# The additions of the norms' squares in GpSimd's program, between the low halves of the weights

## The reference

```python
h = rms_norm(x, norm_g[l, 0]) * (1 + sc1) + sh1
m = even_mixer(h, ...) if l % 2 == 0 else odd_mixer(h, ...)
x = x + g1 * rms_norm(m, norm_g[l, 1])
h = rms_norm(x, norm_g[l, 2]) * (1 + sc2) + sh2
x = x + g2 * rms_norm(mlp(h, mlp_w1[l], mlp_w2[l]), norm_g[l, 3])

def rms_norm(x, g):                       # float32
    y = x * lax.rsqrt(jnp.mean(x * x, axis=-1, keepdims=True) + EPS)
    return y * g
def mlp(h, w1, w2):
    return jnp.square(jax.nn.relu(h @ w1)) @ w2          # 1024 -> 4096 -> 1024
```

## Time and profile before

| what | value |
|---|---|
| time, median of 3 runs | 3595.27 us (3594.14 to 3598.88) |
| profiled execution | 3591.43 us, of which the span of the instructions 3589.8 us |
| TensorE matmul busy | 3171.7 us (88%), mean granted clock 0.927 |
| VectorE busy | 1320.4 us (37%) |
| ScalarE busy | 951.1 us (26%) |
| GpSimd busy | 628.1 us (17%) |

### The profile page before, as it was taken

One profiled execution on the slowest core, in us unless ns is written; L12 is line 12 of the kernel. 1 busy time (PEld: TensorE's weight loads), 2 busy tenths in 40 slices (PEclk: granted clock), 3 DMA queues, 4 the chain that ended last, 5 costly groups with the idle time before them and its releaser, 6 DMA issues. The chain is left out here.

```text
span 3589.8 us, 44989 instructions
## 1 busy us (share of the span) xinstructions
PE 3171.7 (88%) x17605; PEld 2783.1 (78%) x17605; DVE 1320.4 (37%) x2055; ACT 951.1 (26%) x1404; POOL 628.1 (17%) x368
## 2 busy tenths in 40 slices
PE   4898888889777688899999998879778899999998
PEld 2883333369656478899999998867568899999997
DVE  4126651111297417322222227119516422222225
ACT  3016663200231224212122223213324212222211
POOL 1211111121000021221112221117021112222210
PEclk7899999989889589999999999989779999999998
DMA  5110005421231232111111122130242111111112
GB/s 210 53 48 20 1 25 175 153 65 47 100 107 54 78 109 74 48 42 36 40 47 47 47 85 70 52 109 5 66 128 67 43 45 47 47 47 47 41 36 106
DMA packets 236954, 238.89 MB, mean 67 GB/s; under 512 B 8003, under 2 KB 194807, under 8 KB 236565
## 3 DMA queue, kind: packets, MB, share of 16 engines
q1 hardware_dynamic: 221701, 205.73, 18.2%
q0 software_dynamic: 5120, 16.78, 1.5%
q10 hardware_dynamic: 10016, 14.78, 1.2%
HBM read 207.74 MB, written 29.99 MB: 66 GB/s over the span
## 5 line engine op out<-in xcount | busy, mean ns | idle before, releaser
L614 PE MATMUL PS<-trunk_x_hi,trunk_w_hi 128*128 128x364 f32 x2208 | 739.1, 335 | 87.1 <-DVE trunk_x_lo L1242 31.9
L615 PE MATMUL PS<-trunk_x_lo,trunk_w_hi 128*128 128x364 f32 x2208 | 736.3, 333 | 0.0
L616 PE MATMUL PS<-trunk_x_hi,trunk_w_lo 128*128 128x364 f32 x2208 | 735.2, 333 | 0.0
L831 POOL TENSOR_TENSOR trunk_w_lo<-trunk_w_raw,trunk_w_hi 128x1024 fp32r<-128x1024 f32 x128 | 307.0, 2398 | 1318.4 <-ACT trunk_w_hi L1009 1228.1
L614 PE MATMUL PS<-hidden,trunk_w_hi 128*128 128x364 f32 x1536 | 508.0, 331 | 0.0
L615 PE MATMUL PS<-hidden,trunk_w_hi 128*128 128x364 f32 x1536 | 505.9, 329 | 0.0
L616 PE MATMUL PS<-hidden,trunk_w_lo 128*128 128x364 f32 x1536 | 505.5, 329 | 0.0
L614 PEld LDWEIGHTS PS<-trunk_x_hi,trunk_w_hi 128*128 128x128 f32 x2208 | 423.6, 192 | 89.2 <-DVE trunk_x_lo L1242 32.4
L615 PEld LDWEIGHTS PS<-trunk_x_lo,trunk_w_hi 128*128 128x128 f32 x2208 | 423.7, 192 | 0.0
L616 PEld LDWEIGHTS PS<-trunk_x_hi,trunk_w_lo 128*128 128x128 f32 x2208 | 422.8, 191 | 0.0
L1260 DVE TENSOR_TENSOR M<-M,PS 128x364 f32<-128x364 f32 x336 | 178.3, 532 | 440.9 <-PE PS L616 440.9
(11 more groups left out here) (369 smaller groups left out, 4266.3 us busy)
## 6 DMA issues: line engine op xcount, KB each, us to landing
trunk_w_raw<-mlp_w SPq DMA_DIRECT2D x128, 512.0 KB
M<-cache_sb_k SPq DMA_DIRECT2D x64, 256.0 KB, 3.0
big<-cache_sb_v POOLq DMA_DIRECT2D x64, 256.0 KB, 3.3
x_scratch<-x_new ACTq DMA_DIRECT2D x9, 1456.0 KB, 5.9
hgrn_pairs_ada_w<-ada_w SPq DMA_DIRECT2D x24, 512.0 KB
x_new<-x_scratch SPq DMA_DIRECT2D x6, 1456.0 KB, 11.8
trunk_x_old<-x_scratch SPq DMA_DIRECT2D x6, 1456.0 KB, 10.9
setup_ada_w<-ada_w SPq DMA_DIRECT2D x16, 512.0 KB, 7.2
```

The lines of the kernel that those rows point to most:

```text
L614: pe.matmul(out, hi, xh, start=first, stop=False)
L615: pe.matmul(out, hi, xl, start=False, stop=False)
L616: return pe.matmul(out, lo, xh, start=False, stop=last)
L831: pool.tensor_tensor(wl[:, u % 4, :], raw[:, u % 2, :], wh[:, u % 4, :].bitcast(F32), ALU.subtract).then_inc(s_lo, 1)
```

## The change

The function `tree` moves from VectorE's program to GpSimd's, with the same two additions on the same data, the same waits and the same semaphores; all 21 calls go with it (six in each stretch of layer 0 and in the first of layer 1, three at the end). GpSimd's loop over the MLP's groups starts at group 1 instead of 0, and group 0's eight units are written out, with trees in between.

```diff
--- before.py
+++ after.py
@@ -823,15 +823,45 @@
                 pool.tensor_tensor(wl[:, u % 4, :], raw[:, u % 2, :], wh[:, u % 4, :].bitcast(F32),
                                    ALU.subtract).then_inc(s_lo, 1)
 
+            def tree(j, n, c):
+                w = squares_of(j, n, c)
+                pool.wait_ge(s_q[j][n], (c + 1) * (2 if n else 1))
+                pool.tensor_tensor(w[:, 0:4], w[:, 0:4], w[:, 4:8], ALU.add).then_inc(s_tree[j][n], 1)
+                pool.wait_ge(s_tree[j][n], 2 * c + 1)
+                pool.tensor_tensor(w[:, 0:2], w[:, 0:2], w[:, 2:4], ALU.add).then_inc(s_tree[j][n], 1)
+
             for u in range(8):
                 low_weights(u)
-            with pool.Fori(0, G) as g:
+            tree(0, 0, 0)
+            tree(0, 1, 0)
+            tree(0, 0, 1)
+            for u in range(8, 12):
+                low_weights(u)
+            tree(0, 0, 2)
+            tree(0, 1, 1)
+            tree(0, 1, 2)
+            for u in range(12, 16):
+                low_weights(u)
+            with pool.Fori(1, G) as g:
                 for u in range(8):
                     pool.wait_ge(s_hi, g * 8 + (8 + u + 1))
                     pool.tensor_tensor(wl[:, u % 4, :], raw[:, u % 2, :], wh[:, u % 4, :].bitcast(F32),
                                        ALU.subtract).then_inc(s_lo, 1)
-            for n in range(units_next):
-                low_weights(8 + 8 * G + n)
+            u0 = 8 + 8 * G
+            tree(1, 0, 0)
+            if final:
+                tree(1, 0, 1)
+                tree(1, 0, 2)
+                return
+            tree(1, 1, 0)
+            tree(1, 0, 1)
+            for n in range(4):
+                low_weights(u0 + n)
+            tree(1, 0, 2)
+            tree(1, 1, 1)
+            tree(1, 1, 2)
+            for n in range(4, units_next):
+                low_weights(u0 + n)
 
         @block.tensor
         def _(pe):
@@ -1178,13 +1208,6 @@
 
         @block.vector
         def _(dve):
-            def tree(j, n, c):
-                w = squares_of(j, n, c)
-                dve.wait_ge(s_q[j][n], (c + 1) * (2 if n else 1))
-                dve.tensor_tensor(w[:, 0:4], w[:, 0:4], w[:, 4:8], ALU.add).then_inc(s_tree[j][n], 1)
-                dve.wait_ge(s_tree[j][n], 2 * c + 1)
-                dve.tensor_tensor(w[:, 0:2], w[:, 0:2], w[:, 2:4], ALU.add).then_inc(s_tree[j][n], 1)
-
             def recip(j, n, c):
                 dve.wait_ge(s_rt[j][n], c + 1)
                 at = slice(NBK * n + 4 * c, NBK * n + 4 * c + 4)
@@ -1268,12 +1291,9 @@
                 dve.wait_ge(s_sh, c + 1)
                 dve.tensor_tensor(col(XL, c), col(M, c), col(XH, c).bitcast(F32), ALU.subtract).then_inc(s_sl, 1)
 
-            tree(0, 0, 0)
             recip(0, 0, 0)
             scaled(0, 0)
             residual(0, 0)
-            tree(0, 1, 0)
-            tree(0, 0, 1)
             recip(0, 1, 0)
             normed(0, 0)
             recip(0, 0, 1)
...
@@ -1351,9 +1365,7 @@
                     dve.wait_ge(s_rT, i + 1)
                     dve.tensor_copy(rows_of(i)[0:n_rows(i), HALF:D], PS[0:n_rows(i), 2 * (i % 3) + 1, :]).then_inc(s_rv, 1)
                 return
-            tree(1, 1, 0)
             down(e, 2, 0)
-            tree(1, 0, 1)
             down(e, 2, 1)
             recip(1, 1, 0)
...
```

More of the change, by code:

```diff
@@ L1284, in _ @@
             hidden(0, 0, 0)
-            tree(0, 1, 1)
             hidden(0, 0, 1)
-            tree(0, 0, 2)
             hidden(0, 0, 2)
@@ L1297, in _ @@
             hidden(0, 1, 0)
-            tree(0, 1, 2)
             hidden(0, 1, 1)
@@ L1320, in _ @@
                 down(e, 0, f)
-            tree(1, 0, 0)
             down(e, 1, 0)
@@ L1345, in _ @@
                 down(e, 2, 7)
-                tree(1, 0, 2)
                 recip(1, 0, 2)
@@ L1370, in _ @@
             residual(1, 1)
-            tree(1, 1, 1)
-            tree(1, 0, 2)
             recip(1, 1, 1)
@@ L1379, in _ @@
             residual(1, 2)
-            tree(1, 1, 2)
             recip(1, 1, 2)
```

## The result

| | median, us | runs | ratio to before, 95% interval |
|---|---|---|---|
| before | 3597.07 | 3594.14 to 3604.61, 4 | |
| after | 3658.59 | 3651.55 to 3666.03, 4 | 1.0172 (1.0151 to 1.0193) |

Before has one run more here than in the table of its profile. The change makes the kernel 61.5 us slower, 1.7%; 55.5 us and with them 3650 were forecast.

A forecast was written before the change was run, and what follows sets the result against it. A tile-to-tile norm chain was taken to bound the kernel, with the trees' latency on it, not VectorE's load. 23.0 + 22.7 + 9.8 = 55.5 us on 3591.43 gave 3646.9, with the median's 3.8 about 3650; range 3628 to 3663.

The forecast's parts named there:

- more standing: Rival: VectorE's hidden-row steps also stand beside trees (0,1,1), (0,1,2) and reach TensorE's wait; +10 us, 3660; chance 0.11.
- The price of a tree: One tree's two adds on GpSimd: 3.25 and 1.89 us, 5.29 in place of 2.67, so 2.6 later on the path.
- (a): Nine trees (numbered block half, norm, tile) without slack cost their own added latency, 2.4 to 2.6 us each: 23.0 us.
- (b): Three trees, (0,1,1) in two layers and (1,1,1) in the first, pay a stopped residual plus their own latency: 22.7 us.
- the hold: Row tile 1's residual on VectorE stops while GpSimd adds run beside it: 4.9 us in two layers, 4.5 once.
- Standing still: A VectorE instruction with two SBUF inputs stops while GpSimd computes; read from one residual step of 2.75 us beside 0.52.
- sharing: Rival: VectorE and GpSimd both go on, each slower, when they meet; 15 us less, 3635; chance 0.13.
- (c): Nine trees with slack, such as (0,0,1), (0,0,2), (0,1,2), cost nothing; up to 0.5 us each if (0,1,2)'s cover fails.
- (d): TensorE's clock falls behind seven sums with longer stalls: 1.4 us each, 9.8 us; bounds 0 and 12.6.
- the 0.5 that I named as a sign: Granted TensorE clock of the half tile behind the first sums should be 0.5.
- (e): GpSimd's low halves behind the trees: a 2.4 us delay is covered, so no cost.
- Not slower: Rival: delays vanish in TensorE's 31.9 us of low-row waits; 3591, if first sums start within 2.72 us of squares; chance 0.03.

The follow-up runs named there:

- e5_fill_long: The changed kernel plus useless matmuls on TensorE, enough to reach nearly to the end of the late trees: 3642.00 us, 1.0109 of before.
- e3_hold: The kernel before with only three trees on GpSimd, (0,0,2) in both layers and (1,0,2) in layer 0: 3622.12 us, 1.0064 of before.
- e1_swap: The changed kernel with (0,1,1) ahead of (0,0,2) and (1,1,1) ahead of (1,0,2) on GpSimd: 3651.48 us, 1.0133 of before.
- e2_hidden: The kernel before with only the nine trees forecast as free on GpSimd, (0,0,2) and (1,0,2) held back: 3599.64 us, 0.999 of before.

## Why the prediction was right, and which term was not

Direction and size held: 3650 in 3628 to 3663, measured 3658.59. That it lies inside the range is in part luck: with the clock's upper bound of 12.6 the sum is 3653 at most, and the rest of the room, 10 us, was kept for more standing, which was not paid. Step by step:

- **The price of a tree** held: 3361 and 1802 ns for 3.25 and 1.89 us, 5.25 us from squares to first sums for 5.29. The 1.89 of the earlier trace rows had a VectorE instruction running beside its start; alone the second addition takes 1.71 to 1.75, the first 3.25 to 3.36.
- **(a), 23.0 us.** In e5_fill_long, where little but lateness is left, the nine sums are late, each against the step before it, by 2.7 and 2.9 for (0,0,0), 2.7 twice for (0,1,0), 2.7 and 2.8 for (1,0,0), 2.6 for (1,1,0), and 2.5 each for the last two: 24.1 us.
- **(b), 22.7 us.** 7.2, 7.2 and 6.8, 21.2 us in the same run. The two parts were told apart: the hold is 4.6, 4.2 and 4.6 (e3_hold) where 4.9, 4.9 and 4.5 were forecast, and goes when the order is turned (e1_swap); the rest is the tree. Standing still was the right reading of the one step of 2.75 us; sharing, 15 us less, was wrong. The contention that the Trainium skill names in "GPSIMD Engine Reference", section "8. Key points", is there, and in this kernel it is a full stop: 4.59 us lost to 5.57 us of adds, and each step that was held ended 0.4 us after its add.
- **(c), 0.** Right, shown by e2_hidden.
- **(d), 9.8 us, at most 12.6: the mis-sized term.** (a) and (b) measure 45.3 us together, so what is left of the profiled 68.4 is 23.1 us, and of the medians' 61.5 it is 16. Both are above my upper bound. I charged 1.4 us once behind each of seven sums, and nothing behind (0,1,1), since half clock stood there already. The seven came to 8.8 us, near the 9.8, but unevenly: in each layer 1.2 behind (0,0,0), at a clock of 0.67 in the stretch and not the 0.5 that I named as a sign, 0.1 behind (0,1,0), where the clock stayed at 1.00, and 1.6 behind (1,0,0); and 3.1 behind (1,1,1). What failed is the nothing behind the long stall of (0,1,1): the steps from those sums on are late by 1.5, 1.1, 2.7 and 0.8 us, 6.1 in each layer, as the next half tiles, sums and spreads alternate at the low level. With that stall filled up to 0.58 us (e5_fill_long) it is 0.5 and 0.7 in the two layers. The remaining 2 us or so of the profiled 23.1 lie at the end of layer 1 and between the stretches.
- **(e), 0.** The wait for low halves didn't grow (29.5 us for 31.2).
- **Rivals.** "More standing" happens but isn't paid: a hidden row took 2.79 us beside the tree (0,1,1), while TensorE stood for that tree anyway, and the long waits for low rows didn't change. "Not slower" fell at the point named: the first sums start 5.25 us behind their squares, and those waits shrank by nothing.

The total lay 8.6 us below the measured one: 6.0 of these are the change, 61.5 for 55.5, because the term of the clock was short by 6 to 13 us; the rest is the median of before, 1.8 higher than the one that I started from, and rounding.

## What to carry to other kernels

Look for the order of an engine's long instructions against its neighbour's: two adds on an idle engine cost twice where they landed on another engine's residual, and in the trace turning two trees round took that away. A stall of TensorE can cost its length plus the slow matmuls behind it: here 6.1 us more behind one of 8.62 us, and 0.1 to 1.6 behind those of 2.1 to 2.5. So count the second price for stalls that grow, not only for those that are new. Where a wait can't be shortened, matmuls without use in it may pay, but only up to the wait's end and only where the trace shows that wait.

## What the runs showed of the hardware

- The granted clock stayed at 0.50 for over 20 us after a stall of 8.62 us, through half tiles in which TensorE was busy without a gap, with sums, spreads and a wait of 2.33 us between them; after 2.45 us it was 0.67 over 3 us.
- Standing, and not the small matmuls, brings it: the first sums had 1.00 behind them with fillers up to their start, and 0.57 with 0.89 us of standing. It doesn't bring it every time: 2.10 us ahead of (0,1,0) left 1.00, 0.58 us ahead of (0,1,1) was followed by 0.50.
- GpSimd and VectorE hold each other up both ways: an add that began while a VectorE step with two SBUF inputs was running took 3.64 us, alone 3.25 to 3.36; a VectorE step that began beside an add took 2.79 in place of 0.53.
